# Local attention of the far groups: two heads per step instead of one

## The reference, cut to what matters

```python
ATTN_GROUPS = ((128, 1), (512, 4), (2048, 16))     # window, dilation
for gi, (win, dil) in enumerate(ATTN_GROUPS):
    o_g, lse_g = dilated_window_attention(qa[:, :, gi], ka[:, :, gi], va[:, :, gi], win, dil)
# in dilated_window_attention, per block of queries and head:
scores = jnp.einsum('brhnqd,brhnkd->brhnqk', qb, kb) * (dh ** -0.5)
scores = jnp.where(valid, scores, -jnp.inf)
m = jnp.max(scores, axis=-1, keepdims=True)
e = jnp.exp(scores - m)
denom = jnp.sum(e, axis=-1)
o = jnp.einsum('brhnqk,brhnkd->brhnqd', e, vb) / denom[..., None]
```

## Time and profile before

| | us |
|---|---|
| median of 3 runs | 3278.3 |
| lowest and highest | 3276.19, 3284.53 |
| the profiled execution | 3278.68 |
| its span in the trace | 3276.9 |
| PE busy | 2985.7 (91%) |
| DVE busy | 1706.9 (52%) |
| ACT busy | 1256.7 (38%) |

### The profile page before, as it was taken

One profiled execution on the slowest core, in us unless ns is written; L12 is line 12 of the kernel. 1 busy time (PEld: TensorE's weight loads), 2 busy tenths in 40 slices (PEclk: granted clock), 3 DMA queues, 4 the chain that ended last, 5 costly groups with the idle time before them and its releaser, 6 DMA issues.

```text
span 3276.9 us, 35421 instructions
## 1 busy us (share of the span) xinstructions
PE 2985.7 (91%) x13998; PEld 2333.0 (71%) x13998; DVE 1706.9 (52%) x2469; ACT 1256.7 (38%) x1913; POOL 14.8 (0%) x22
## 2 busy tenths in 40 slices
PE   7997899999999988899999999998679779969997
PEld 5465677888885656677888887766357567858886
DVE  3346435555433464445554335446665445449995
ACT  3133233433231333234332224445343524348883
POOL 0000000000000000000000000000000000000000
PEclk9999999999998989899999999999889889989998
DMA  4111112233331111122233331111011012358981
GB/s 157 39 36 49 54 33 91 93 97 97 94 122 58 46 36 56 38 65 97 97 97 104 104 101 56 57 55 46 32 38 40 28 43 69 102 195 341 396 339 58
DMA packets 96180, 307.70 MB, mean 94 GB/s; under 512 B 25744, under 2 KB 31760, under 8 KB 84240
## 3 DMA queue, kind: packets, MB, share of 16 engines
q1 hardware_dynamic: 69056, 284.88, 25.5%
q10 hardware_dynamic: 24368, 11.12, 1.2%
q0 software_dynamic: 2592, 9.44, 0.8%
HBM read 296.49 MB, written 8.91 MB: 93 GB/s over the span
## 4 chain that ended last, share of the span: by engine, by line
PE 79%; DVE 9%; ACT 5%; issue 4%; DMA 2%; ACTq 1%; POOL 0%; POOLq 0%; DVEq 0%
PE bank L370 19%; PE bank L371 18%; PE bank L372 18%; PE bank L365 2%; PE bank L367 2%; PE bank L366 2%; ACT flow_head L389 2%; DVE flow_rest L400 1%; PE bank L1911 1%; PE bank L1993 1%; PE bank L2023 1%; PE bank L546 1%; PE bank L556 1%; PE bank L2444 1%; PE bank L1214 1%
## 5 line engine op out<-in xcount | busy, mean ns | idle before, releaser
L370 PE MATMUL bank<-h_head,flow_head 128*128 128x512 f32 x2144 | 906.3, 423 | 28.7 <-DVE flow_rest L400 24.3
L400 DVE TENSOR_TENSOR flow_rest<-flow_raw,flow_head 128x1024 fp32r<-128x1024 f32 (+2 forms) x372 | 438.5, 1179 | 944.0 <-ACT flow_head L389 944.0
L371 PE MATMUL bank<-h_rest,flow_head 128*128 128x512 f32 x2144 | 849.9, 396 | 0.0
L372 PE MATMUL bank<-h_head,flow_rest 128*128 128x512 f32 x2144 | 849.0, 396 | 0.0
L389 ACT ACTIVATE flow_head<-flow_raw 128x1024 fp32r<-128x1024 f32 (+2 forms) x372 | 379.2, 1020 | 732.9 <-PE bank L372 685.3
L370 PEld LDWEIGHTS bank<-h_head,flow_head 128*128 128x128 f32 x2144 | 412.7, 193 | 157.7 <-issue 70.3
L371 PEld LDWEIGHTS bank<-h_rest,flow_head 128*128 128x128 f32 x2144 | 412.3, 192 | 91.0 <-issue 16.3
L372 PEld LDWEIGHTS bank<-h_head,flow_rest 128*128 128x128 f32 x2144 | 410.9, 192 | 89.7
L370 PE MATMUL bank<-ff_head,flow_head 128*128 128x512 f32 x352 | 136.9, 389 | 0.0
L371 PE MATMUL bank<-ff_rest,flow_head 128*128 128x512 f32 x352 | 136.9, 389 | 0.0
L372 PE MATMUL bank<-ff_head,flow_rest 128*128 128x512 f32 x352 | 136.9, 389 | 0.0
(11 more groups left out here) (603 smaller groups left out, 4353.7 us busy)
## 6 DMA issues: line engine op xcount, KB each, us to landing
flow_raw<-in_w_in SPq DMA_DIRECT2D x176, 512.0 KB, 3.4
ring<-in_experts SPq DMA_DIRECT2D x84, 1024.0 KB, 7.2
flow_raw<-in_w_gate_up SPq DMA_DIRECT2D x88, 512.0 KB, 3.4
flow_raw<-in_w_down SPq DMA_DIRECT2D x32, 512.0 KB, 3.6
flow_raw<-in_w_out SPq DMA_DIRECT2D x24, 512.0 KB, 3.5
flow_raw<-in_paths SPq DMA_DIRECT2D x24, 256.0 KB, 2.6
flow_raw<-in_w_down SPq DMA_DIRECT2D x16, 384.0 KB, 3.1
flow_raw<-in_path_b SPq DMA_DIRECT2D x8, 512.0 KB, 3.5
```

The source lines that it names most:

```text
L370: nc.tensor.matmul(ps[u.bank][:, :], wh[:, c:c + P], head, start=start, stop=False)
L371: nc.tensor.matmul(ps[u.bank][:, :], wh[:, c:c + P], rest, start=False, stop=False)
L372: last = nc.tensor.matmul(ps[u.bank][:, :], wr[:, c:c + P], head, start=False, stop=stop)
L400: nc.vector.tensor_tensor(self.parts_of[p.slot][1][:, 0:p.words], p.raw, f32(self.parts_of[p.slot][0][:, 0:p.words]), ALU.subtract).then_i ...
```

## The change

Only the far groups change; near keeps the old loops. PE gets five steps of two heads. logit_two(c) issues the four blocks' scores of both heads in turn (head 0 in bank 0, head 1 in bank 1), and apply_two(c) does the same with the value products, in the lower and the upper half of bank 4. The flow is called at the middle and the end of a step. On ACT a step is the values' copy of the chunk before, the stream up to the middle, both keeps, both softmaxes, the stream to the end. On DVE the two masks of a chunk stand next to each other, and the copy out of bank 4 comes at the end of the step. The products, their number and their operands are the same.

```diff
@@ -2025,17 +2025,56 @@
                                         start=j == 0, stop=(m + 1 == len(tiles) or tiles[m + 1][0] != b), skip_group_check=True)
             last.then_inc(*applied.up())
 
-        for u in range(U + 2):
-            if u < U:
-                logit(u)
-            flow.pe(at((u + .4) / (U + 2)))
-            if 0 <= u - 1 < U:
-                turn(u - 1)
-            if u >= 2:
-                apply(u - 2)
-            if u % 2 and u // 2 < 4:
-                values(u // 2)
-            flow.pe(at((u + 1) / (U + 2)))
+        def logit_two(c):
+            if c == 0:
+                pe.wait_ge(*k.qk_done.at(8))
+            else:
+                pe.wait_ge(*masked.at(2 * c))
+            for b in range(4):
+                for h in range(2):
+                    r = slice(h * HD, (h + 1) * HD)
+                    last = nc.tensor.matmul(ps[h][:, b * P:(b + 1) * P], q[r, c, b * P:(b + 1) * P], kk[r, c, b * P:(b + 1) * P],
+                                            start=True, stop=True)
+                    if b == 3:
+                        last.then_inc(*logits.up())
+
+        def apply_two(c):
+            pe.wait_ge(*kept.at(2 * c + 2))
+            pe.wait_ge(*v_kept.at(c + 1))
+            if c:
+                pe.wait_ge(*k.win_done.at(4 * g + c))
+            for b in range(4):
+                for h in range(2):
+                    last = nc.tensor.matmul(ps[4][h * HD:(h + 1) * HD, b * P:(b + 1) * P], v_tok[:, b, h * HD:(h + 1) * HD],
+                                            pt[:, h, b * P:(b + 1) * P], start=True, stop=True, skip_group_check=True)
+                    if b == 3:
+                        last.then_inc(*applied.up())
+
+        if near:
+            for u in range(U + 2):
+                if u < U:
+                    logit(u)
+                flow.pe(at((u + .4) / (U + 2)))
+                if 0 <= u - 1 < U:
+                    turn(u - 1)
+                if u >= 2:
+                    apply(u - 2)
+                if u % 2 and u // 2 < 4:
+                    values(u // 2)
+                flow.pe(at((u + 1) / (U + 2)))
+        else:
+            for c in range(5):
+                if c < 4:
+                    logit_two(c)
+                flow.pe(at((c + .5) / 5))
+                if c < 4:
+                    values(c)
+                if c:
+                    turn(2 * c - 2)
+                    turn(2 * c - 1)
+                flow.pe(at((c + 1) / 5))
+                if c:
+                    apply_two(c - 1)
 
     def vector_part():
         def mask(u):
@@ -2060,7 +2099,8 @@
         for u in range(U + 2):
             if u < U:
                 mask(u)
-            flow.dve(at((u + .9) / (U + 2)))
+            if near or u % 2:
+                flow.dve(at((u + .9) / (U + 2)))
             if u >= 2 and u % 2:
                 c = (u - 2) // 2
                 v.wait_ge(*applied.at(u - 1))
@@ -2088,18 +2128,33 @@
                 last = nc.scalar.activation(pt[:, u % 2, 0:512], ps[2 + u % 2][:, :], ACT.Copy)
             last.then_inc(*kept.up())
 
-        for u in range(U + 2):
-            if u < U:
-                softmax(u)
-            if 0 <= u - 1 < U:
-                keep(u - 1)
-            if u % 2 and u // 2 < 4:
-                c = u // 2
-                a.wait_ge(*v_turned.at(c + 1))
+        def keep_values(c):
+            a.wait_ge(*v_turned.at(c + 1))
+            if c:
+                a.wait_ge(*applied.at(2 * c))
+            nc.scalar.activation(v_tok[:, :, :], blocks(ps[5][:, :]), ACT.Copy).then_inc(*v_kept.up())
+
+        if near:
+            for u in range(U + 2):
+                if u < U:
+                    softmax(u)
+                if 0 <= u - 1 < U:
+                    keep(u - 1)
+                if u % 2 and u // 2 < 4:
+                    keep_values(u // 2)
+                flow.act(at((u + 1) / (U + 2)))
+        else:
+            for c in range(5):
                 if c:
-                    a.wait_ge(*applied.at(2 * c))
-                nc.scalar.activation(v_tok[:, :, :], blocks(ps[5][:, :]), ACT.Copy).then_inc(*v_kept.up())
-            flow.act(at((u + 1) / (U + 2)))
+                    keep_values(c - 1)
+                flow.act(at((c + .5) / 5))
+                if c:
+                    keep(2 * c - 2)
+                    keep(2 * c - 1)
+                if c < 4:
+                    softmax(2 * c)
+                    softmax(2 * c + 1)
+                flow.act(at((c + 1) / 5))
 
     tensor_part()
     vector_part()
```

## The result

| us | before | changed |
|---|---|---|
| median of 6 runs | 3279.9 | 3269.1 |
| lowest and highest | 3276.2, 3286.2 | 3256.8, 3275.8 |
| ratio of the two, 95% interval | | 0.9947, 0.9928 to 0.9965 |
| the profiled execution, its span | 3278.7, 3276.9 | 3275.8, 3274.0 |

The changed kernel is faster, as forecast, by 11 us between the medians and by 17 us (0.0053 x 3280) by the ratio. The forecast was 21.6 us. The median lies 3 us above the range of the prediction; the ratio applied to 3278.3 us, 3261, lies inside it.

What follows compares the result with a forecast made beforehand. PE was taken to bound group 1 and the first half of group 2, ACT and DVE in turn the second half. 3278.7 - 11.6 - 10.0 = 3257.1, forecast 3257 us, range 3253 to 3262.

Steps and rivals of the forecast that it cites:

- the range of the prediction: Whole kernel: 3253 to 3262 us, given a chance of 0.70.
- Scores: PE, each far group: 16 score instructions of two heads cost 1.29 us, as eight did, saving 5.1 us.
- The upper bound taken from L1058: Scores in each far group: all instructions pair as at L1058, saving 5.1 us; 1.6 us if nothing pairs.
- Value products: apply_two on PE: column halves pair, so two heads cost 1.22 us; 6.1 us less in group 1.
- Group 1: PE bounds this stretch: scores -5.1, value products -6.1, merged borders -0.4, in all -11.6 us.
- the slower rival: Eight steps with softmaxes: L389 behind ACT's block makes PE wait 4 us a step, 3289 us; chance 0.03.
- Group 2: ACT and DVE decide its second half; the mix begins at 57.5 instead of 67.5 us, -10.0 us.
- the walk: Group 2's queues on PE, ACT and DVE, stepped through from measured spacings, put the mix's start at 57.5 us.
- the last sentence of the sum: Behind group 2: what follows the mix shifts with its start, so no gain is lost there.
- a weak gain in group 2: ACT and DVE hardly gain: group 2 gains 0 to 4 us, total 3263 to 3267 us; chance 0.10.
- the scores alone: Only scores pair: group 1 loses 2.7 us of its gain, group 2 about 1; 3261 us; chance 0.04.

Runs made afterwards that it cites:

- the finer version: Changed kernel with ACT's block in group 2 opened for the stream between softmaxes and DVE's masks apart; median 3253.3 us, ratio 0.9909; run again 3256.1 us, 0.9931.
- the repeat: The changed kernel once more, word for word; median 3266.2 us, ratio 0.9955 to the kernel before.

## Why the prediction came out as it did

- **Scores.** Right. Two heads cost 1.30 us, forecast 1.29. The upper bound taken from L1058 was the value.
- **Value products.** Right. Column halves pair: 16 in 1.09 us. The Trainium skill ("TensorE: Matmul & The Clock Gate", Part 3, Packing small matmuls) says that a weight load overlaps with products under way only when its row group differs. This case's trace disagrees, already before the change: the weights of one of L2023's products load from 2124.62 to 2124.76 us, within the product before it, which runs from 2124.62 to 2124.89 us and uses the same 128 rows. That apply_two would then keep 16 spacings was my inference (group 1 would have gained 2.7 us less), not the page's: the same Part 3 of the Trainium skill lists a measured gain for column tiles.
- **Group 1.** 69.5 us, forecast 69.5; 11.7 gained. The fourth apply_two is hidden in the wait for the squares, which shrank by 1.0 us (forecast 1.2). No wait of PE inside the group but the 0.17 us at its first scores, and none for weight rests, so the slower rival, the starving by splits, didn't come.
- **Group 2.** Right, 10.3 gained of a forecast of 10.0. PE waits for L1785 and for the keeps, where the walk put it. That the order on ACT and DVE binds it is confirmed by the finer version: with the same work of PE it takes 4.6 us less once ACT's block is opened.
- **A gain not forecast.** The norm and group 2 together take 88.6 and 89.0 us in the two profiles of before, 87.6 with group 1 alone changed and 77.3 in the changed kernel, which is 11.3 less than 88.6. So 1.0 us comes on top of the 10.3, in the norm, where the clock is back at 2.4 GHz 1.9 us earlier. The stages sum up to 23.0 us; the forecast had 21.6.
- **The step that failed** is the last sentence of the sum: "What follows the mix hangs on its start and shifts with it." It does start earlier, and 8.6 us of the gain are lost behind the restart, where the clock stays at 1.2 GHz for 50.9 us and not 7.4. The profile of before shows low pieces of 13.6 us at both restarts; I took their length as fixed, a term put at nothing without a reason, and priced no case in which it changes. The long piece doesn't follow from the new loops, since the old ones show it too; what makes it long is open, with the moment of the restart as the best supported account. By the stages it would be 3278.7 - 23.0 + 8.6 = 3264.3, and the repeat's median is 3266.2.
- **The range.** It was built from the unknown costs of the two groups, which gained 22.0 of a forecast 21.6 us; for the clock it had nothing. The 8.6 us lost behind the restart used up the room that was meant for a weak gain in group 2. By the ratio (3261) and by the stages (3264.3) the kernel lies inside the range, by the median of its six runs 3.1 us outside; that it holds by two of three measures is luck. Runs of one program differ by up to 19 us here (3256.8 to 3275.8), more than the whole range. Its chances also don't add up as said: 0.70, 0.10, 0.05 and the 0.04 of the scores alone lie inside, which leaves out 1 in 10 and not 2.

## What to carry to other kernels

In this kernel small products of two heads that use different halves of the array cost together what one costs (1.30 and 1.29 us); put them next to each other and in turn, and price the change from a place in the same trace where halves already alternate. Where a stage alternates between two engines, walk their queues from measured spacings: it gave the end of group 2 to 0.3 us. And where PE takes up work again behind a long wait, look at how long its clock is low there in several profiles before promising that a gain ahead of it arrives at the end; compare kernels by their stages, since the sum also holds the luck of the clock.

## What the hardware did that I had not expected

- At a restart after 10 to 21 us of waiting PE's clock was back at 2.4 GHz after 6.7 to 11.5 us in seven profiles and after 35.5 to 53.9 us in six, with PE busy 37.68 of 37.70 us in the long case. The same instructions behind it take 24.3 to 26.3 us or 36.7 to 37.6 us. One program (before with 1.2 us added) showed both, with the restart 10.3 and 7.5 us after the clock's fall.
- Two heads' instructions that are not in turn still pair at their border: 0.54 us dearer than in turn, not 0.88.
- 1.2 us of work added to a wait in the kernel before cost 7.5 and 15.0 us between the medians, in two sets of runs.
